# One decoder layer on one core: the bias row's product and tables, the gains' loads, K's evacuation and the place of the FFN transposes are moved

## The reference: what is computed

```python
h = rmsnorm(x, pre_mix_norm)
rq, rk, rv, rg, mq, mk, mv = split(h @ w_in)         # 1024 x 3072
ret = silu(rg) * head_rmsnorm(retention(rotary(rq), rotary(rk) / 8, rv))       # 4 heads
moba = softmax(mq @ mk.T / 8 + bias[t5_bucket(i - j)], causal) @ mv            # 8 heads of 64
x = x + rmsnorm(concat([ret, moba]) @ w_out, post_mix_norm)
h = rmsnorm(x, pre_ffn_norm)
f = (silu(h @ w_gate) * (h @ w_up)) @ w_down         # d_ff = 2816
x = x + rmsnorm(f, post_ffn_norm)
```

## Time and profile before

| what | value |
|---|---|
| median of 3 runs | 316.71 us (316.2 to 316.86) |
| the profiled execution | 318.91 us |
| its span | 317.1 us |
| its mean granted clock of PE | 0.998 |
| PE busy in the span | 305.3 us |
| DVE busy | 182.7 us |
| ACT busy | 153.3 us |
| POOL busy | 27.6 us |

### The profile page before, as it was taken

The page is one execution under the profiler, slowest core; times in us unless marked ns, Lnnn a source line. Parts: engine busy times, 40 slices in busy tenths (PEclk is TensorE's granted clock), DMA queues, the critical chain, the costliest instruction groups (busy, mean ns, idle before and its releaser), DMA issues.

```text
span 317.1 us, 4124 instructions
## 1 busy us (share of the span) xinstructions
PE 305.3 (96%) x1432; PEld 248.8 (78%) x1432; DVE 182.7 (58%) x255; ACT 153.3 (48%) x254; POOL 27.6 (9%) x31
## 2 busy tenths in 40 slices
PE   7999987999999999999999999999999999999992
PEld 3788866888888888768888888888888888888881
DVE  2858265697467487899555555544444454551426
ACT  4889626446608174676444444444433333340322
POOL 4021056000002000540000000000000000000001
PEclk9999999999999999999999999999999999999999
DMA  6999974314541543169965555555566565400003
GB/s 216 398 407 373 413 308 134 134 66 153 180 144 57 198 156 111 66 231 317 367 203 179 179 190 180 168 184 191 198 198 198 198 196 183 149 0 0 0 2 132
DMA packets 17517, 58.35 MB, mean 184 GB/s; under 512 B 1997, under 2 KB 2517, under 8 KB 17504
## 3 DMA queue, kind: packets, MB, share of 16 engines
q1 hardware_dynamic: 17136, 57.06, 51.6%
q0 software_dynamic: 368, 1.11, 1.0%
HBM read 57.10 MB, written 1.06 MB: 183 GB/s over the span
## 4 chain that ended last, share of the span: by engine, by line
PE 85%; DVE 7%; ACT 3%; DMA 2%; POOL 2%; issue 1%; SPq 0%; DVEq 0%
PE bank L951 25%; PE bank L953 24%; PE bank L952 24%; PE bank L961 4%; DVE w_lo L681 2%; DMA raw<-in_w_in 2%; PE bank L978 1%; POOL xs L437 1%; PE bank L982 1%; PE bank L986 1%; ACT w_hi L451 1%; DVE d_lo L876 1%; ACT kz L518 1%; PE bank L1049 1%; DVE res L942 1%
## 5 line engine op out<-in xcount | busy, mean ns | idle before, releaser
L951 PE MATMUL bank<-w_hi,a_hi 128*128 128x512 f32 x256 | 101.9, 398 | 0.0
L953 PE MATMUL bank<-w_hi,a_lo 128*128 128x512 f32 x256 | 100.1, 391 | 0.0
L952 PE MATMUL bank<-w_lo,a_hi 128*128 128x512 f32 x256 | 99.6, 389 | 0.0
L617 ACT ACTIVATE sil<-bank,rstd 128x256 f32<-128x256 f32 x22 | 10.4, 473 | 96.1 <-PE bank L953 93.7
L953 PEld LDWEIGHTS bank<-w_hi,a_lo 128*128 128x128 f32 x256 | 48.0, 188 | 10.6
L952 PEld LDWEIGHTS bank<-w_lo,a_hi 128*128 128x128 f32 x256 | 48.2, 188 | 9.8
L951 PEld LDWEIGHTS bank<-w_hi,a_hi 128*128 128x128 f32 x256 | 48.1, 188 | 9.4
L869 DVE TENSOR_TENSOR w_lo<-raw,w_hi 128x1024 fp32r<-128x1024 f32 x40 | 49.6, 1276 | 6.7 <-ACT w_hi L602 6.7
L681 DVE TENSOR_TENSOR w_lo<-raw,w_hi 128x1024 fp32r<-128x1024 f32 x32 | 42.2, 1345 | 19.4 <-ACT w_hi L451 19.4
L884 DVE SCALAR_TENSOR_TENSOR hid<-bank,rstd,sil 128x256 f32<-128x256 f32 x22 | 10.7, 485 | 73.9 <-ACT sil L617 73.9
L602 ACT ACTIVATE w_hi<-raw 128x1024 fp32r<-128x1024 f32 x40 | 40.5, 1057 | 0.5 <-DMA raw<-in_w_gu 0.5
(11 more groups left out here) (119 smaller groups left out, 307.5 us busy)
## 6 DMA issues: line engine op xcount, KB each, us to landing
raw<-in_w_gu SPq DMA_DIRECT2D x44, 512.0 KB, 4.3
raw<-in_w_dn SPq DMA_DIRECT2D x22, 512.0 KB, 4.6
raw<-in_w_in SPq DMA_DIRECT2D x20, 512.0 KB, 8.5
raw<-in_w_out SPq DMA_DIRECT2D x8, 512.0 KB, 3.2
raw<-in_w_in SPq DMA_DIRECT2D x8, 256.0 KB, 5.8
xs<-in_x SPq DMA_DIRECT2D x2, 512.0 KB, 8.6
bias<-bias_row POOLq DMA_DIRECT2D x1, 1024.0 KB, 10.2
out<-res SPq DMA_DIRECT2D x4, 256.0 KB, 2.0
```

The source lines that it names most:

```text
L617: act.activation(sil[:, t, :], pg[:, t, 0:FG], ACT.Silu, scale=rstd[:, X1_, t:t + 1]).then_inc(sil_ready[t], 1)
L951: pe.matmul(acc, hi, wh, start=first, stop=False)
L952: pe.matmul(acc, hi, wl, start=False, stop=False)
L953: return pe.matmul(acc, lo, wh, start=False, stop=last)
```

## The change

- **Bias row.** PE makes its product before all projections. `bucket` and `rel` are loaded from ACT's queue, as its first instructions, and no longer from POOL's.
- **Gains.** SP issues `gp` after piece 10 and `gm` after piece 11.
- **Evacuations.** `qn`, `kn` and `v` stand ahead of the `hi_in` of their step on ACT.
- **K.** ACT writes `kz` for the even heads (2 instructions), DVE for the odd heads (2 instructions), ahead of its `lo_in` of step 10. The scores of head 0 wait for both.
- **FFN.** A group on PE is now `gate_up(g, 0)`, `gate_up(g, 1)`, `down(g - 1, 0)`, both `turn_hidden(g, t)`, `down(g - 1, 1)`. It was `gate_up(g, 0)`, `turn_hidden(g - 1, 1)`, `down(g - 1, 0)`, `gate_up(g, 1)`, `turn_hidden(g, 0)`, `down(g - 1, 1)`. Group 0 is turned in the middle of `gate_up(1, 1)`; for this `gate_up(1)` goes into bank45 and the transposes of group 0 into bank01. On ACT and DVE the parts of `hid` follow: `h_hi_part(g, 1)` and `h_lo_part(g, 1)` open the next group.

```diff
@@ -159,8 +159,13 @@
         ph = bank45
-        pg = bank01
-        pt = bank45
+
+        def pg(g):
+            return bank45 if isinstance(g, int) and g == 1 else bank01
+
+        def pt(g):
+            return bank01 if isinstance(g, int) and g == 0 else bank45
+
         pf = [bank67, bank23]
@@ -348,9 +354,9 @@
                     sp.dma_start(decay[:, :, :], decay_c).then_inc(decay_loaded, 16)
-                if n == 16:
+                if n == 10:
                     sp.dma_start(gp[:, :], g_pre_ffn.broadcast_to([P, D])).then_inc(gp_loaded, 16)
-                if n == 18:
+                if n == 11:
                     sp.dma_start(gm[:, :], g_post_mix.broadcast_to([P, D])).then_inc(gm_loaded, 16)
@@ -398,8 +404,6 @@
             pool.wait_ge(half_ready, 1)
-            pool.dma_start(rel[0:BUCKETS, :], rel_bias).then_inc(rel_loaded, 16)
-            pool.dma_start(bucket[:, :], bucket_c).then_inc(rel_loaded, 16)
@@ -462,6 +466,8 @@
+            act.dma_start(bucket[:, :], bucket_c).then_inc(rel_loaded, 16)
+            act.dma_start(rel[0:BUCKETS, :], rel_bias).then_inc(rel_loaded, 16)
             act.wait_ge(half_ready, 1)
@@ -513,11 +519,17 @@
                         act.wait_ge(k_turned, t + 1)
-                        for odd in range(2):
-                            rows = slice(64 * odd, 64 * odd + 64)
-                            act.activation(kz[rows, odd:MH:2, t * P:(t + 1) * P],
-                                           wk[rows, t, :].rearrange("p (b i) -> p b i", i=P), ACT.Copy
-                                           ).then_inc(kT_ready, 1)
+                        act.activation(kz[0:64, 0:MH:2, t * P:(t + 1) * P],
+                                       wk[0:64, t, :].rearrange("p (b i) -> p b i", i=P), ACT.Copy
+                                       ).then_inc(kT_ready, 1)
+                if u == UPG:
+                    act.wait_ge(nq_ready, 1)
+                    wait_factor(act, X_, NT - 1)
+                    rows_out(qn, 0, lambda t: nq[:, t:t + 1], q_nat)
+                if u == 2 * UPG:
+                    rows_out(kn, 1, r_x, k_nat)
+                if u == 3 * UPG:
+                    rows_out(v, 2, r_x, v_nat)
                 hi_in(u + LEAD)
@@ -527,14 +539,6 @@
                         squares(X_, u, c, xs[:, u, c * CW:(c + 1) * CW])
-                if u == UPG:
-                    act.wait_ge(nq_ready, 1)
-                    wait_factor(act, X_, NT - 1)
-                    rows_out(qn, 0, lambda t: nq[:, t:t + 1], q_nat)
-                if u == 2 * UPG:
-                    rows_out(kn, 1, r_x, k_nat)
-                if u == 3 * UPG:
-                    rows_out(v, 2, r_x, v_nat)
                 if u == RQK_T + 1:
@@ -614,23 +618,27 @@
                     act.wait_ge(hid_ready[t], g)
-                act.activation(sil[:, t, :], pg[:, t, 0:FG], ACT.Silu, scale=rstd[:, X1_, t:t + 1]
+                act.activation(sil[:, t, :], pg(g)[:, t, 0:FG], ACT.Silu, scale=rstd[:, X1_, t:t + 1]
                                ).then_inc(sil_ready[t], 1)
                     wait_down(act, g - 1, t)
-                act.activation(h_hi[:, t, :, :], pt[:, t, 0:FG].rearrange("p (b i) -> p b i", i=P),
+                act.activation(h_hi[:, t, :, :], pt(g)[:, t, 0:FG].rearrange("p (b i) -> p b i", i=P),
                                ACT.Copy).then_inc(hhi_ready[t], 1)
+                if g0 > 1:
+                    h_hi_part(g - 1, 1)
                 if more:
                 silu(g, 0)
-                h_hi_part(g - 1, 1)
+                if g0 == 1:
+                    for t in range(NT):
+                        h_hi_part(0, t)
                 if more:
@@ -651,7 +659,6 @@
             silu(0, 1)
-            h_hi_part(0, 0)
             hi_dn(0, 1, 0)
@@ -739,6 +746,12 @@
             for u in range(N_IN):
+                if u == K_T + 1:
+                    for t in range(NT):
+                        dve.wait_ge(k_turned, t + 1)
+                        dve.tensor_copy(kz[64:P, 1:MH:2, t * P:(t + 1) * P],
+                                        wk[64:P, t, :].rearrange("p (b i) -> p b i", i=P)
+                                        ).then_inc(kT_odd, 1)
                 if 0 <= u - (S0 + 1) < MH:
@@ -881,21 +894,25 @@
                     dve.wait_ge(h_turned[t], g)
-                dve.scalar_tensor_tensor(out=hid[:, t, :], in0=pg[:, t, FG:2 * FG],
+                dve.scalar_tensor_tensor(out=hid[:, t, :], in0=pg(g)[:, t, FG:2 * FG],
                                          scalar=rstd[:, X1_, t:t + 1], in1=sil[:, t, :],
                 dve.wait_ge(hhi_ready[t], g + 1)
-                dve.tensor_tensor(h_lo[:, t, :, :], pt[:, t, 0:FG].rearrange("p (b i) -> p b i", i=P),
+                dve.tensor_tensor(h_lo[:, t, :, :], pt(g)[:, t, 0:FG].rearrange("p (b i) -> p b i", i=P),
                                   h_hi[:, t, :, :].bitcast(F32), ALU.subtract).then_inc(hlo_ready[t], 1)
             def group(g, g0, more=True):
+                if g0 > 1:
+                    h_lo_part(g - 1, 1)
                 if more:
                 hidden(g, 0)
-                h_lo_part(g - 1, 1)
+                if g0 == 1:
+                    for t in range(NT):
+                        h_lo_part(0, t)
                 if more:
@@ -916,7 +933,6 @@
             hidden(0, 1)
-            h_lo_part(0, 0)
             lo_dn(0, 1, 0)
@@ -967,6 +983,11 @@
                 pe.matmul(bank67[:, 0, :], zeros[:, 0:P], zeros[:, 0:CW], start=True, stop=True)
+
+            pe.wait_ge(rel_one, 1)
+            pe.wait_ge(rel_loaded, 32)
+            pe.matmul(wk[0:MH, 0, 0:REV], rel[:, :], bucket[:, :], start=True, stop=True
+                      ).then_inc(brow_done, 1)
@@ -1020,12 +1041,6 @@
-                if u == 1:
-
-                    pe.wait_ge(rel_one, 1)
-                    pe.wait_ge(rel_loaded, 32)
-                    pe.matmul(wk[0:MH, 0, 0:REV], rel[:, :], bucket[:, :], start=True, stop=True
-                              ).then_inc(brow_done, 1)
                 if u == Q_T:
@@ -1042,7 +1057,8 @@
                         pe.wait_ge(kz_zeroed, 2)
-                        pe.wait_ge(kT_ready, 2 * NT)
+                        pe.wait_ge(kT_ready, NT)
+                        pe.wait_ge(kT_odd, NT)
                     else:
@@ -1142,7 +1158,7 @@
-                if not (isinstance(g, int) and g == 0):
+                if not (isinstance(g, int) and g <= 1):
                     pe.wait_ge(hid_ready[t], g)
@@ -1152,7 +1168,7 @@
                             pe.wait_ge(alo_ready, 2 * t + k // 4 + 1)
-                        ins = product(pg[:, t, :], a_hi[:, k, tile(t)], a_lo[:, k, tile(t)],
+                        ins = product(pg(g)[:, t, :], a_hi[:, k, tile(t)], a_lo[:, k, tile(t)],
                                       w_hi[:, a0 % RING, i * CW:(i + 1) * CW],
@@ -1167,7 +1183,7 @@
                     pe.wait_ge(hlo_ready[t], g)
-                turn(pt[:, t, :], hid[:, t, :], DN, h_turned[t])
+                turn(pt(g)[:, t, :], hid[:, t, :], DN, h_turned[t])
@@ -1190,12 +1206,17 @@
+            def first_hidden(s):
+                if s == 1:
+                    for t in range(NT):
+                        turn_hidden(0, t)
+
             def group(g, g0):
-                gate_up(g, 0, g0)
-                turn_hidden(g - 1, 1)
+                for t in range(NT):
+                    gate_up(g, t, g0, hook=first_hidden if g0 == 1 and t == 1 else None)
                 down(g - 1, 0, g0 - 1)
-                gate_up(g, 1, g0)
-                turn_hidden(g, 0)
+                for t in range(NT):
+                    turn_hidden(g, t)
                 down(g - 1, 1, g0 - 1)
@@ -1204,13 +1225,11 @@
             gate_up(0, 1, 0)
-            turn_hidden(0, 0)
             group(1, 1)
             group(NF - 1, NF - 1)
-            turn_hidden(NF - 1, 1)
             down(NF - 1, 0, NF - 1, last=True)
```

More of the change, by code:

```diff
@@ L211, in hybrid_layer @@
         kT_ready = sem("kT_ready")
+        kT_odd = sem("kT_odd")
         kz_zeroed = sem("kz_zeroed")
```

## The result

| | median | runs | lowest to highest |
|---|---|---|---|
| before | 316.75 us | 4 | 316.2 to 316.86 |
| changed | 319.98 us | 4 | 319.75 to 322.22 |

The ratio is 1.0113, with a 95% interval from 1.0074 to 1.0152. The predicted 316.3 us, and its range up to 317.9, did not hold. The mean granted clock of PE is 0.986 to 0.991 in the four runs of the changed kernel, and 0.994 or more in 80 of the 83 runs of the kernel before that stand beside the experiments.

A forecast was written before the change was run, and what follows sets the result against it. PE, busy 305.3 of 317.1 us, was taken as the bound, so only its stream and waits count. Terms -0.4 (to head 3), +0.2 (FFN start) and -0.2 (steady groups) gave -0.4, so 316.3 us on the median; range 313.9 to 317.9.

The forecast's parts named there:

- The queue of POOL and DVE: Before head 0: three POOL products and four DVE w_lo take turns from 29.74 to 41.0 us; scores at 42.2.
- The rival that POOL holds DVE up for less: Before head 0: K's odd half ready between 39.5 and 40.5, wait 1 to 2 us, total 313.7 to 314.8; chance 22%.
- the one of gains that land late: Rival at POOL's products: gm lands late, lengthening the chain; two microseconds late give +1.6, 318.3 us; chance 18%.
- Which makes one of 3.5 us: PE at the scores: waits at heads 2 and 3 go, one of 3.5 us at head 0 comes; head 3 0.4 earlier.
- the wait of PE passes 5 us: Within the late-gains rival (18%): PE's clock might fall; at 1.2 GHz a 12-matmul unit would cost 2.7 us more.
- The change goes onto the median: Whole kernel: profiled execution stands 2.2 us above the median 316.71, so the -0.4 was applied to the median: 316.3 us.
- Bias row: PE's start: product free in an early wait, later units gain 0.74 us, 0.6 left behind Q's transposes.
- Start of the FFN: First FFN groups on PE: 0.8 us wait goes, 1.3 us wait for hid(1, 1) comes; +0.2 us, bounds 0 to +0.6.
- Steady groups: Ten later FFN groups: three changes between kinds of work instead of four; -0.2 us, between 0 and -0.45.

The follow-up runs named there:

- the experiment with unused matmuls: Changed kernel with 16 unused matmuls of 512 columns in PE's wait at head 0: 318.49 us, ratio to before 1.0044.
- the FFN alone: Kernel before with only the FFN's new order: 316.50 us, ratio 0.9971.
- the bias row alone: Kernel before with only the bias row's product ahead of all projections and its tables on ACT's queue: 316.22 us, ratio 0.9956.
- the products behind the split: Kernel before with POOL's products waiting for ACT's w_hi of unit 16, its two memsets ahead of them: 317.09 us, ratio 0.9966.
- late products: Kernel before with POOL's three products behind the last logits and its two memsets ahead of them: 315.35 us, ratio 0.9941.
- K's odd half on ACT: Changed kernel, gains still early, with all four copies of K on ACT as before: 317.35 us, ratio 1.0.

## Why the prediction was wrong, step by step

- **The queue of POOL and DVE: right.** Head 0's scores were put at 42.2 us and came at 42.42; the products at near 30 and came at 29.70; the four `w_lo` were to end at 41.0 and ended at 40.94. The sum let DVE go on without a gap. In the trace it stood 2.40 us for the split of a late piece, and this cost nothing beside the products, since POOL's second product ran in that time. The rival that POOL holds DVE up for less fell, and so did the one of gains that land late. The Trainium skill (SBUF — State Buffer, Who interferes with whom) calls the shared port pair an exclusive lock; in this case's traces the `w_lo` of 1.98 us, which came into a product, and the first of the two at 36.38, 3.43 us, beside 1.23 undisturbed, agree.
- **"Which makes one of 3.5 us": the clock behind it is the first step that failed.** The wait was 3.77 us, and the text let the clock fall only in the rival where "the wait of PE passes 5 us". It fell behind 3.77, and cost 1.57 us in the trace and 1.5 in the medians of the experiment with unused matmuls. The forecast reasoned from waits up to 1.78 us, which could bound nothing above them. Without the fall of the clock head 3 would be at 54.55 - 1.57 = 52.98; 52.8 was forecast. The Trainium skill (TensorE: Matmul & The Clock Gate, What's actually happening) says that an idle TensorE falls back to the lower clock. The trace of the changed kernel agrees, by the granted clock of 0.50 behind the wait.
- **"The change goes onto the median": the second step that failed.** The 3.2 us of waits in the earlier trace rows, which the wait at head 0 was set against, exist in full only in the longer kind of execution, 22 of 83. In the usual one, by the traces of three kernels that differ little from it (the FFN alone, the bias row alone, the products behind the split), the first of them is not there and the second is 1.2 to 1.5 us; late products gain 1.5 to 1.6 us on it, which fits. The change removes both in either kind and pays 3.77 + 1.57 us each time, so on the usual execution it loses what the profiled one hides: 318.91 - 316.71 = 2.2 us. The two orders of POOL and DVE, 0.3 us apart in the earlier trace rows, were the sign.
- **Bias row: right in size, and hidden in the changed kernel.** 0.74 was expected at first and 0.6 behind Q's transposes. In the experiment of its own 0.54 to 0.81 was left at head 0, by which trace of before it is held against, and 0.6 to 0.7 in the median; that can't tell 0.6 from 0.74. In the changed kernel it lies ahead of the wait at head 0, which swallows it.
- **Start of the FFN: +0.42 against +0.2,** within its bounds. The forecast's own terms give 153.8 - 153.25 - 0.22 = +0.33. `hid(1, 1)` ends the wait as forecast, 0.89 us, and a `w_lo` adds 0.3 (the waits above).
- **Steady groups: -0.8 against -0.2, outside the bound of -0.45.** From `down(0, 1)` to the end the difference goes from +1.62 to +0.81, about 0.07 a group. The mechanism is only in part that of the text: in the trace before the matmuls of the half group behind 184.10 us start (188.94 - 184.55) / 19 = 0.231 us apart and then (192.57 - 188.94) / 16 = 0.227. So a change of kind costs not one gap but some hundredths spread over the 19 matmuls behind it. Why is open.

In one sum, on the medians: -0.4 forecast; +2.2 for the kind of execution; +1.6 for the clock; +0.1 at head 3, -0.1 behind it; -0.4 for the FFN; +0.2 by which the changed kernel's median is above its profiled execution. That is +3.2, as measured (319.98 - 316.75).

Two things are open. One is what moves POOL's start: it was 43.37 us in both traces of the kernel before, and 44.17 in that of the FFN alone, which is the same program up to there; that it moves so within the kernel before is not shown. The other is whether shorter waits bring the clock down. The traces show no fall behind waits up to 1.8 us and one behind 3.77. But beside the three runs of K's odd half on ACT, three of the 83 of the kernel before, 320.65 to 320.75 us, have a mean granted clock of 0.991 to 0.993 and are 1.5 to 1.6 us above that kind's median of 319.14, about the price of one fall.

## What to carry to other kernels

A profiled execution that stands above the median is a finding and no offset: look in it for two engines that begin within some tenths of each other at a shared resource, and cost the change for both orders. A wait that gathers several small ones in one place has to be priced with PE's clock behind it, 1.57 us here. Work that nobody waits for, like these products, belongs where the engine it blocks has nothing due; that was worth 1.6 us. Moving its loads earlier cost 3.8 us, in part by the products and in part by the pieces behind the loads, and that much only with K's odd half on DVE: alone in the kernel before it gave 317.15 us against 316.73, which can't be told from none.

## What was unexpected of the hardware

- PE's clock went to 1.2 GHz for about 3.4 us near the end of 3.77 us of idleness, and stayed at 2.4 GHz when 16 matmuls of unused data filled 3.79 us of it (clock 0.50 and 1.00 in 42.2 to 45.5 us).
- Two kinds of execution of one program, some 2.3 us apart (medians of 316.80 and 319.14 us) with nothing between, came from whether POOL's first product or a DVE instruction was first: with the order fixed by a wait, 12 of 12 runs were of the shorter kind.
- A half group's matmuls start 0.231 us apart behind transposes and a change of weights, and 0.227 later, at the same clock.
